# One layer's sample compressor in a two-layer transformer kernel: three half-width products for two neighbouring blocks in place of four, with the differences made by GpSimd and VectorE in turn

## Chip, cores and metric

One core of a Trainium2 chip runs the whole program as one launch. The metric is the device time of that launch in microseconds (us), lower is better. TensorE is PE below and its weight loads PEld; VectorE is DVE, ScalarE is ACT, GpSimd is POOL, SyncE is SP.

## What is computed

The program is one forward pass of a small two-layer model on 1024 prompt tokens and on 8 samples of 4 new tokens with 2048 cached positions each. The change lies in the second (odd) layer, in the part for the samples: sparse attention with compressed blocks. The cached keys and values of a sample are cut into blocks of 32 positions, one every 16, and each block goes through a small network:

```python
per = CMP_LEN // CMP_STRIDE                      # 32 // 16 = 2
n_cmp = (t - CMP_LEN) // CMP_STRIDE + 1          # 127 blocks for 2048 positions
pieces = kv[:, :CMP_STRIDE * (n_cmp + per - 1)].reshape(n, n_cmp + per - 1, CMP_STRIDE, g, hd)
blocks = jnp.concatenate([pieces[:, j:j + n_cmp] for j in range(per)], axis=2)
hid = silu(einsum('nilgd,ldf->nigf', blocks + pos_emb, w1.reshape(CMP_LEN, hd, CMP_HIDDEN)))
return einsum('nigf,fd->nigd', hid, w2)          # (n, 127, 2 groups, 64)
```

So with pieces x[i] of 16 positions, hidden block i is A x[i] + B x[i+1] plus a bias, where A and B are the two halves of w1 (each 1024 x 256), for keys and for values with weights of their own. The queries attend the compressed blocks; their probabilities choose which 64-position blocks of the cache are attended in full; a window of the last 512 positions is attended too; the three results are mixed by gates.

## The kernel before

`build` runs stages one after the other, each a set of five instruction streams (one for each engine) with semaphores between them. The stage of this change is `attend_samples_sparse` (L2886). It comes after the second layer's input projection (`project_out`, L1246 and L1259 are its products), and is followed by the prompt's attention of that layer.

**Items and steps.** The 8 samples go in 4 pairs p (PAIRS, L2888). For each pair there are two items: m = 0 compresses the keys, m = 1 the values, in the order K0 V0 K1 V1 K2 V2 K3 V3. An item has 8 steps l (KD), one for every two of the 16 positions in a piece: 2 positions x 64 dims fill the 128 rows of the contraction. The moving operand of a step is `x` of 512 columns: 2 samples x 2 groups x 128 pieces. Float32 numbers are cut into a high and a low part (`hi`, `lo`, type fp32r), and a product is three matmuls: hi x lo, lo x hi, hi x hi.

**PE.** `hidden(m, p, hh)` (L3210) is one of 16 half-steps hh of an item: l = hh // 2 is the step and c = hh % 2 the half of the 256 hidden units. It issues six matmuls of 128x512 (L3229), three for A and three for B, where B reads the same x one column further on (x[:, s:s + XW]). An item is 96 of them, the stage 768. Before step l it waits for `x_cut` (L3223); after the last half-step of a step it gives `x_used`.

**What is done between half-steps.** After each half-step PE does a piece of the other work of the pair, written out by hand: `turn(what, p, x)` transposes (ks: the selected-branch keys, L3182; win: the window's, L3186; pc, psel, pwin, pnew: probabilities, L3195 to L3207) at the slots of the tables TURNS_K and TURNS_V (L2895); `down_k`, `compressed_scores`, `scores` (into two PSUM banks by turns, L3236) at hh 1 to 4 of the V item; the sums that choose blocks at hh 7 and 8; `down_v` and `times_v` (L3282, the probabilities times the values, L3299 to L3310) at hh 1 and 4 of the next pair's K item. The streams of ACT and DVE follow the same slots in the same order, so a wait on one of them holds all that stands behind it there.

**How x is made.** Step t = item x 8 + l is made three steps ahead (`step_ahead`, L2914, at even hh). DVE turns it (`turn_x`, two transposes of 128x256, L3080) into one of two buffers `x_raw`; ACT copies it to `x_hi` (`take_x_high`, L3087), for which it waits until PE is done with the step four back (`x_used`); DVE then makes `x_lo` = x_raw - x_hi (`take_x_low`, L3093). In `take_x_low(t)` DVE first turns step t + 1, then waits for `x_high` of t.

**POOL** issues the gathers from the paged caches: eight indirect DMAs (L3032) for each item, into one of two buffers, and four (L3021) for each pair for the selected-branch keys and values. It also scales the probabilities (L3159 twice, L3160) when DVE has made the coefficients (`coef_ready`, L3572).

**The chain of the selected branch** in the V item: `select(p)` at hh 8 on DVE (choose blocks, then add the mask over 2048 scores, L3507), an exponential on ACT at hh 11 (L3427), reciprocals on DVE at hh 12 (L3572), scaling on POOL (L3159), and PE turns psel 0 and 1 at hh 15 (L3200).

**Start.** ACT and DVE cut the weights of the keys (L3393, L3522; `low_weights(0)`), and later those of the values (`low_weights(1)`); both sets stay in SBUF for the whole stage. Meanwhile PE compresses the prompt's own pieces (`comp.hidden`, L2867), and POOL issues the first gathers. The bias and the silu are one ACT instruction from PSUM for each half c (`silu`, L3367).

Of the kernel before, what the change touches and what calls it, by code (L numbers as in the profile page):

```python
# [14 lines left out]
F32 = mybir.dt.float32  # L15
# [3 lines left out]
ALU = mybir.AluOpType  # L19
# [34 lines left out]
def _constants():  # L54
# [48 lines left out]
    c, b = np.arange(NCS)[:, None], np.arange(NSL)[None, :]  # L103
# [1220 lines left out]
class SparseLoads:  # L1324


    def __init__(self, nc, ctx, constants, h, turned, mix_s, comp):
# [12 lines left out]
        self.o_stored = ctx.semaphore("ss_stored")  # L1340
        self.k_in = [c[:, :, :].rearrange("p s c -> p (s c)").rearrange("p (t g a d) -> p t g a d", t=NT, g=2, a=2) for c in self.c_in]
# [1544 lines left out]
def attend_samples_sparse(nc, constants, comp, following, h, kcmp, vcmp, pools, wins, gates, mix_s):  # L2886

    PAIRS = NB // 2  # L2888
    NKEY = PAST + NJ
    HALVES = 2 * KD  # L2890
    AHEAD, N_X = 3, 4
    XW = 4 * P
    N_STEPS = 2 * PAIRS * KD
    R2 = 2 * 64
    TURNS_K = {0: [("psel", 2), ("psel", 3)], 1: [("pwin", 0)], 2: [("pnew", 0)], 5: [("win", 0)], 6: [("win", 1)]}  # L2895
    TURNS_V = {6: [("pc", 0)], 15: [("psel", 0), ("psel", 1)]}
    for q in range(6):
        TURNS_K.setdefault(10 + q, []).append(("ks", q))
    TURNS_K[15].append(("new", 0))
    for q in range(6, 8):  # L2900
        TURNS_V.setdefault(q - 6, []).append(("ks", q))

    def turns_of(m, p, hh):

        turns = []
        for what, x in (TURNS_V if m else TURNS_K).get(hh, ()):
            if what in ("pwin", "pnew") or what == "psel" and m == 0:
                if p:
                    turns.append((what, p - 1, x))
            else:  # L2910
                turns.append((what, p, x))
        return turns

    def step_ahead(m, p, hh):  # L2914

        n = (2 * p + m) * KD + hh // 2 + AHEAD
        return n if hh % 2 == 0 and n < N_STEPS else None

    LAST_TURNS = [("psel", PAIRS - 1, 2), ("psel", PAIRS - 1, 3), ("pwin", PAIRS - 1, 0), ("pnew", PAIRS - 1, 0)]
# [6 lines left out]
    for p in range(PAIRS):  # L2926
        for m in range(2):
            for hh in range(HALVES):
                for x in turns_of(m, p, hh):
                    enter(*x)  # L2930
    for x in LAST_TURNS:
        enter(*x)
# [4 lines left out]

    def hidden_count(m, p, c):
        return (2 * p + m) * 2 + c + 1

    with Phase(nc) as ctx:
# [11 lines left out]
        x_raw = [sb(f"x_raw{b}", [P, XW]) for b in range(2)]  # L2953
# [8 lines left out]
        kc, vc = w_flat[1][:, 2048:2048 + 2 * NCS].rearrange("p (a b) -> p a b", a=2), w_flat[1][0:NCS, 3336:3592].rearrange("c (a k) -> c a k", a=2)  # L2962
# [3 lines left out]
        w_hi, w_lo = ([sb(f"{n}{m}", [P, 16, CH], F32R) for m in range(2)] for n in ("w_hi", "w_lo"))  # L2966
        x_hi, x_lo = ([sb(f"{n}{b}", [P, XW + 2], F32R) for b in range(N_X)] for n in ("x_hi", "x_lo"))
        hid = [sb(f"hid{m}", [P, 2, 2, 2, NCS]) for m in range(2)]
        ksT = [comp.lent[:, a * PAST:(a + 1) * PAST] for a in range(2)]
        newT = sb("newT", [P, 2, 2, NJ])  # L2970
        pc, pn, pcT = sb("pc", [R2, NCS]), sb("pn", [R2, NCS]), sb("pcT", [NCS, R2])
# [4 lines left out]
        o, o_cmp = following.o, sb("o_cmp", [R2, P])  # L2976
        ps_t = [ctx.enter_context(nc.psum_tensor(f"ss_ps_t{b}", [P, 512], F32)) for b in range(2)]
        ps_s = [ctx.enter_context(nc.psum_tensor(f"ss_ps_s{b}", [P, 512], F32)) for b in range(2)]
# [45 lines left out]
        def gather_items(pool, f):  # L3024
            b = f % 2
            if f >= 2:
                pool.wait_ge(x_turned, (f - 1) * KD)
            for a in range(2):
                if f == 1 and a == 1:
                    comp.landing.wait(pool)  # L3030
                for q in range(4):
# [659 lines left out]
```

## Time and profile before

| what | value |
|---|---|
| median of three runs | 1787.94 us (1786.65 to 1789.09) |
| span of the profiled execution | 1786.0 us |
| PE busy over the span | 1725.0 us |
| DVE, ACT, POOL busy | 892.8, 695.8, 418.0 us |
| the stage's products of x run from | 978.1 to 1245.1 us of the span |
| DMA | 245.31 MB, mean 137 GB/s |

The span runs from the first to the last instruction of the program; the time of a run also has what lies around it, here 1.9 us from the profile's span to the median. A row of the profile names the line of the kernel, the engine, the operation and the tiles (out<-in), with shapes as partitions x elements. PE's records overlap, since matmuls are pipelined, so the pace of a run of matmuls is read from their starts and not from their durations.

### The profile page before, as it was taken

The numbers are of one execution on the slowest core, as the hardware profiler recorded it, in microseconds if no ns is written. First come the engines' busy times: TensorE is split into PE (matmuls) and PEld (weight loads), VectorE is DVE, ScalarE is ACT, GpSimd is POOL, SyncE is SP. The second block draws the span as 40 slices with busy tenths as digits, with TensorE's granted clock in tenths as the row PEclk, the third lists the DMA queues.
The fourth block names the chain that finished last, engine by engine and source line by source line (L and its number), as shares of the span: only waits on it lengthen the run. The fifth ranks groups of instructions, "written<-read, shape, count | busy, mean of one in ns | idle before, by whom it ended". The sixth has DMA issues, their size and how long they took to land. (4 is left out here: it accounts for less than half of the span.)

```text
span 1786.0 us, 34260 instructions
## 1 busy us (share of the span) xinstructions
PE 1725.0 (97%) x13111; PEld 1412.2 (79%) x13111; DVE 892.8 (50%) x2673; ACT 695.8 (39%) x1535; POOL 418.0 (23%) x591
## 2 busy tenths in 40 slices
PE   7999999999899899999999999999799999999998
PEld 5878778678776778887789787787688888888998
DVE  5322222288456445222224555454677787778534
ACT  4200000176332323100112334233687877787413
POOL 0000000000464000000003342331365656565300
PEclk9999999999999999999999999999899999999999
DMA  5443343464889765466434442536400000000154
GB/s 211 147 171 135 141 152 111 148 225 138 258 259 287 258 227 193 116 196 206 135 98 157 161 140 92 196 110 165 119 20 25 26 26 24 22 14 8 59 163 156
DMA packets 148409, 245.31 MB, mean 137 GB/s; under 512 B 34939, under 2 KB 82808, under 8 KB 145944
## 3 DMA queue, kind: packets, MB, share of 16 engines
q1 hardware_dynamic: 132936, 198.48, 34.4%
q0 software_dynamic: 7424, 33.56, 5.5%
q10 hardware_dynamic: 7888, 11.08, 2.1%
q8 instruction: 107, 1.75, 0.4%
q14 instruction: 54, 0.44, 0.1%
HBM read 201.35 MB, written 48.77 MB: 140 GB/s over the span
## 5 line engine op out<-in xcount | busy, mean ns | idle before, releaser
L1998 POOL TENSOR_SCALAR sparse_pr<-sparse_pr,sparse_coef,sparse_gate 128x63 f32<-128x63 f32 (+8 forms) x384 | 247.1, 662 | 160.8 <-DVE sparse_coef L1938 160.8
L1884 ACT ACTIVATE sparse_pr<-sparse_pr,sparse_nmax 128x63 f32<-128x63 f32 (+8 forms) x384 | 227.7, 595 | 67.5 <-DVE sparse_nmax L1932 67.3
L1246 PE MATMUL x_acc<-x_w_hi,x_y_lo 128*128 128x512 f32 (+3 forms) x448 | 157.3, 351 | 1.6 <-DVE x_y_lo L1058 1.4
L1246 PE MATMUL x_acc<-x_w_lo,x_y_hi 128*128 128x512 f32 (+3 forms) x448 | 155.3, 347 | 0.0
L1246 PE MATMUL x_acc<-x_w_hi,x_y_hi 128*128 128x512 f32 (+3 forms) x448 | 154.9, 346 | 0.0
L511 PE MATMUL h_acc<-h_w_hi,h_y_lo 128*128 128x512 f32 x384 | 151.7, 395 | 0.8 <-DVE h_y_lo L433 0.8
L511 PE MATMUL h_acc<-h_w_lo,h_y_hi 128*128 128x512 f32 x384 | 150.1, 391 | 0.0
L511 PE MATMUL h_acc<-h_w_hi,h_y_hi 128*128 128x512 f32 x384 | 149.9, 390 | 0.0
L1805 PE MATMUL sparse_ps<-cmp_lent,ss_pieces 64*128 64x384 f32 (+3 forms) x928 | 136.6, 421 | 5.2 <-DVE sparse_part L1932 3.5
L1817 PE MATMUL sparse_ps<-constants_shared,sparse_pr 128*128 128x128 f32 x1120 | 132.9, 276 | 3.3 <-DVE sparse_nmax L1932 2.2
L458 DVE COPY cmp_w<-h_acc 128x512 f32<-128x512 f32 x48 | 33.2, 691 | 204.6 <-PE h_acc L511 204.6
L1817 PEld LDWEIGHTS sparse_ps<-constants_shared,sparse_pr 128*128 128x128 f32 x1120 | 123.0, 142 | 10.8 <-DVE sparse_nmax L1932 4.7
L1932 DVE CUSTOM_DVE_ANT_0 sparse_pr<-sparse_ps,cmp_w 128x63 f32<-128x63 f32 (+4 forms) x384 | 121.0, 369 | 17.2 <-PE sparse_ps L1805 17.0
L1845 PE MATMUL sparse_ps_o<-sparse_prT,ss_pieces 128*64 128x128 f32 x2112 | 128.6, 273 | 0.0
L3032 POOL DMA_INDIRECT ss_c_in<-in_cache_c_kcmp,cmp_quarters x32 | 34.3, 1071 | 402.2 <-POOLq L168 383.8
L1691 DVE COPY sparse_prT<-sparse_ps 128x384 f32<-128x384 f32 (+1 forms) x152 | 94.1, 621 | 58.1 <-PE sparse_ps L1817 54.5
L1845 PEld LDWEIGHTS sparse_ps_o<-sparse_prT,ss_pieces 128*64 128x64 f32 x2112 | 116.9, 137 | 3.7 <-issue 3.2
L3229 PE MATMUL ss_ps_h<-ss_x_lo,ss_w_hi 128*128 128x512 f32 x256 | 109.7, 429 | 1.0 <-ACT ss_hid L3367 1.0
L2339 POOL MEMSET ev_q_all<- 128x1024 f32 x1 | 1.0, 953 | 464.4 <-POOLq L1694 464.4
L1805 PEld LDWEIGHTS sparse_ps<-cmp_lent,ss_pieces 64*128 64x128 f32 x928 | 73.7, 188 | 40.2 <-issue 14.4
L1932 DVE CUSTOM_DVE_ANT_0 sparse_pr<-sparse_ps,cmp_w,sparse_part 128x128 f32<-128x128 f32 (+3 forms) x208 | 101.0, 526 | 4.1 <-PE sparse_ps L1805 4.1
L3229 PE MATMUL ss_ps_h<-ss_x_hi,ss_w_lo 128*128 128x512 f32 x256 | 102.4, 400 | 0.0
(406 smaller groups left out, 3474.0 us busy)
## 6 DMA issues: line engine op xcount, KB each, us to landing
h_w_side<-in_even_w_in SPq DMA_DIRECT2D x16, 896.0 KB
h<-cmp_w SPq DMA_DIRECT2D x48, 256.0 KB, 2.0
h_w_raw<-in_even_w_in SPq DMA_DIRECT2D x6, 2048.0 KB, 8.9
x_w_side<-in_odd_w_in SPq DMA_DIRECT2D x16, 716.0 KB, 6.7
cmp_lent<-in_odd_w_in SPq DMA_DIRECT2D x5, 2048.0 KB, 9.3
ev_unit<-in_cache_a_k SPq DMA_DIRECT2D x4, 2048.0 KB
ev_unit<-in_cache_a_v SPq DMA_DIRECT2D x4, 2048.0 KB
h_turned<-x_out SPq DMA_DIRECT2D x32, 256.0 KB, 2.7
```

The source lines that it names most:

```text
L458: nc.vector.tensor_copy(outb[:, b, 0:width(i)], acc[b][:, 0:width(i)]).then_inc(evacuated[b], 1)
L511: last = nc.tensor.matmul(acc[b][:, 0:width(i)], rows[:, k, t * P:(t + 1) * P], weights(cols, i)[:, k, :], start=(k == 0 and a == 0), stop ...
L1246: last = nc.tensor.matmul(acc[b][:, 0:passes[p][3]], left[:, k, t * P:(t + 1) * P], weights(right, p)[:, k, :], start=(k == 0 and a == 0), ...
L1691: ins = nc.scalar.copy(to, src) if by_act(what, x) else nc.vector.tensor_copy(to, src)
L1805: ins = nc.tensor.matmul(to[e][:, o:o + b - a], qT[i % 2][half, t * P:(t + 1) * P], rhs, start=True, stop=True)
L1817: last = nc.tensor.transpose(to[:, x:x + P], pr[:, e, at:at + P], con("ident"))
L1845: ins = nc.tensor.matmul(ps_o[e * HD:(e + 1) * HD, cols], lhs, rhs, start=br == segs[0][0] and k == s0, stop=br == segs[-1][0] and k + P > ...
L1884: nc.scalar.activation(row, row, ACT.Exp, scale=-1.0, bias=nmax[u % UB][:, e * NBR + br:e * NBR + br + 1], accum_out=lsum[u % UB][:, e * N ...
L1932: nc.vector.tensor_tensor_reduce(out=row_of(e, a, b, blocks), in0=bank("score", (c, e))[:, o:o + b - a], in1=bias, scale=1.0, scalar=so_fa ...
L1998: nc.gpsimd.tensor_scalar(row, row, one, gate[:, t, 2 * i + e, (br + 1) % 3:(br + 1) % 3 + 1], ALU.mult, ALU.mult).then_inc(scaled, 1)
L3032: pool.indirect_dma_start(out=split[b][a][:, q * 512:(q + 1) * 512], out_offset=None, in_=pools[f % 2].rearrange("r (k c) -> (r k) c", k=4 ...
L3229: ins = nc.tensor.matmul(ps_h[c][:, :], w[m][:, lw, c * P:(c + 1) * P], x[b][:, s:s + XW], start=l == 0 and s == 0 and i == 0, stop=l == K ...
```

## The change

It rewrites how the samples' hidden blocks are made, and the schedule around it.

1. Two neighbouring blocks share a product. With an even piece e = x[2j], the odd one o = x[2j+1] and the next even one e' = x[2j+2], block 2j is A(e - o) + (A+B)o, and block 2j+1 is (A+B)o + B(e' - o). So a step is `both` (kind 2, A+B times o), kind 0 (A times e - o) and kind 1 (B times e' - o), each on 256 columns, for two halves c: 18 matmuls of 128x256 in place of 12 of 128x512.
2. `turn_x` writes even and odd pieces apart. A new `differ` makes the two differences (one instruction with 512 results): on POOL for even steps, on DVE for odd ones. `x_hi` and `x_lo` have 768 columns.
3. `both` has a PSUM bank of its own; ACT copies it out (`take_both`), DVE adds it to the sums of each half (`add_parts`), and ACT's silu works in SBUF on that. `scores` is left with one PSUM bank.
4. The items' order becomes K0 K1 K2 K3 V0 V1 V2 V3. There is one set of cut weights, with three kinds. During item 3 the values' weights replace the keys' in place, step by step: SP loads two 128x256 parts (four DMAs, after the step before is cut), POOL adds them, ACT and DVE cut them.
5. The other work is placed by an explicit table; of a pair p > 0 the compressed scores come in its first item at hh 4, and the mask, exponential, coefficients and scaling at hh 8, 9, 10 and 11 of its second item, psel 0 and 1 at hh 14. `mask` is split from `select`. The sum over selected and window values is copied out (`take_acc`), and the compressed values are added items later (`times_vc`, `out`).

The columns of the constant `overlap` and the block order of the hidden rows are permuted to fit. The core of the diff:

```diff
-    XW = 4 * P
+    XP = 2 * P
+    XO_AT = XP + 8
+    E_AT = XO_AT + XP
+        cmp_item, c0 = (o, 3) if p == 0 else (e, 4)
+        at(cmp_item, c0, "cmp", p)
...
+        for x in range(5):
+            at(o, 3 + x, "scores", p, x)
+        tail = (o, 11) if p == 0 else (o, 8)
...
+        at(*later(0), "mask", p)
+        at(*later(1), "exp", p)
+        at(*later(2), "coef", p)
+        at(*later(3), "scale", p)
+        for x in range(2):
+            turn_at(*later(6), "psel", p, x)
+            turn_at(*later(7), "psel", p, 2 + x)
...
+        at(*later(10), "values", p)
...
+        at(p + 1, 1, "down_k", p)
...
+        def load_next(sp, l):
+            if l:
+                sp.wait_ge(next_cut, l)
+            fr = comp.w1_of[1].rearrange("(s b u p) f -> u b p s f", s=2, b=4, u=8)
+            for b in range(4):
+                sp.dma_start(w_next[32 * b:32 * b + 32, :, :], fr[l, b]).then_inc(next_in, 16)
...
+        def by_pool(t):
+            return t % 2 == 0
+
+        def differ(eng, t):
+            eng.wait_ge(x_turned, t + 1)
...
+            eng_of.tensor_tensor(raw[:, E_AT:E_AT + 2 * XP].rearrange("p (r c) -> p r c", r=2), after, odd, ALU.subtract).then_inc(x_diff[t % 2], 1)
...
+            act.wait_ge(x_diff[t % 2], t // 2 + 1)
...
+            nc.scalar.copy(x_hi[t % N_X][:, :], x_raw[t % 2][:, XO_AT:XO_AT + 3 * XP]).then_inc(x_high, 1)
...
+                def next_sum(l):
+                    pool.wait_ge(next_in, 64 * (l + 1))
...
+                    nc.gpsimd.tensor_tensor(w_next_sum[:, :], w_next[:, 0, :], w_next[:, 1, :], ALU.add).then_inc(next_summed, 1)
...
+                for n, hh in slots():
+                    t = step_ahead(n, hh)
+                    if t is not None and t + 1 < N_STEPS and by_pool(t + 1):
+                        differ(pool, t + 1)
...
+                    if hh >= 7 and hh < 15 and n + 2 < ITEMS:
+                        gather_quarter(pool, n + 2, hh - 7)
+                    if (n, hh) == (PAIRS, 0) or n == PAIRS - 1 and hh >= 2 and hh % 2 == 0:
+                        next_sum(KD - 1 if n == PAIRS else hh // 2 - 1)
...
+                        for c in range(2):
+                            last = product(ps_x[:, c * XP:(c + 1) * XP], 2, c, 0, c == 0, c == 1)
...
+                        product(ps_h[0][:, 0:XP], 0, 0, 1, True, False)
+                    else:
+                        last = product(ps_h[0][:, XP:2 * XP], 1, 0, 2, False, True)
...
+                        product(ps_h[1][:, 0:XP], 0, 1, 1, True, False)
+                        product(ps_h[1][:, XP:2 * XP], 1, 1, 2, False, True).then_inc(x_used, 1)
...
+                def take_both(n):
+                    act.wait_ge(both_done, n + 1)
...
+                    nc.scalar.copy(both_sb[:, :], ps_x[:, :]).then_inc(both_taken, 1)
...
+                def next_high_part(l):
+                    act.wait_ge(next_summed, l + 1)
+                    act.wait_ge(x_used, (PAIRS - 1) * KD + l + 1)
+                    nc.scalar.copy(w_hi[:, l, 0:2, :], w_next[:, :, :])
+                    nc.scalar.copy(w_hi[:, l, 2, :], w_next_sum[:, :]).then_inc(next_high, 1)
...
+                    nc.vector.tensor_tensor(to, own, both, ALU.add).then_inc(summed, 1)
+
+                def next_low_part(l):
+                    dve.wait_ge(next_high, l + 1)
+                    nc.vector.tensor_tensor(w_lo[:, l, 0:2, :], w_next[:, :, :], w_hi[:, l, 0:2, :].bitcast(F32), ALU.subtract)
+                    nc.vector.tensor_tensor(w_lo[:, l, 2, :], w_next_sum[:, :], w_hi[:, l, 2, :].bitcast(F32), ALU.subtract).then_inc(next_cut, 1)
...
+                    if (n, hh) == (PAIRS, 1) or n == PAIRS - 1 and hh >= 3 and hh % 2 == 1:
+                        next_low_part(KD - 1 if n == PAIRS else (hh - 3) // 2)
...
+                nc.vector.tensor_tensor(w_sum, first, second, ALU.add).then_inc(w_summed, 1)
+                for kind, raw in enumerate((first, second, w_sum)):
+                    dve.wait_ge(w_high, kind + 1)
+                    nc.vector.tensor_tensor(w_lo[:, :, kind, :], raw, w_hi[:, :, kind, :].bitcast(F32), ALU.subtract).then_inc(w_cut, 1)
```

A slot (n, hh) below is half-step hh of item n, n from 0 to 7 in the new order; items 2p and 2p + 1 carry the other work of pair p.

## Rows read from the trace of the kernel before

**Rows 1.** The page, busy time by engine: busy us, share of the span, instructions.
```profile
PE 1725.0 (97%) x13111; PEld 1412.2 (79%) x13111; DVE 892.8 (50%) x2673; ACT 695.8 (39%) x1535; POOL 418.0 (23%) x591
```

**Rows 2.** Busy time by stretch: the stage, a V item, a K item; clock, DMA.
```profile
978.00:1246.00 268.00, 265.13 (x1507) 204.66 (x1506) 144.62 (x382) 92.92 (x153) 85.15 (x81) 0.99 0.47 149
1010.00:1043.00 33.00, 33.00 (x162) 24.03 (x161) 19.96 (x60) 14.40 (x23) 6.49 (x6) 1.00 0.18 64
1043.00:1078.00 35.00, 34.60 (x245) 28.45 (x245) 16.38 (x38) 9.01 (x17) 16.98 (x17) 1.00 0.65 212
```

**Rows 3.** Timeline of PE: the first and last of 36 stage products in a row.
```profile
1098.60 0.40 PE L3229 MATMUL ss_ps_h<-ss_x_hi,ss_w_lo 128*128 128x512 f32 x1
...
1106.81 0.40 PE L3229 MATMUL ss_ps_h<-ss_x_lo,ss_w_hi 128*128 128x512 f32 x1
```

**Rows 4.** Timeline of PE: 20 products of 512, 27 of 304 columns; a transposes' row.
```profile
859.64 0.39 PE L1259 MATMUL x_acc<-x_y_hi,x_w_lo 128*128 128x512 f32 x1
...
863.94 0.39 PE L1259 MATMUL x_acc<-x_y_lo,x_w_hi 128*128 128x512 f32 x1
...
939.33 0.30 PE L1246 MATMUL x_acc<-x_w_lo,x_y_hi 128*128 128x304 f32 x1
...
942.92 0.30 PE L1246 MATMUL x_acc<-x_w_hi,x_y_lo 128*128 128x304 f32 x1
...
1108.23 1.04 PE L3200 MATMUL ss_ps_t<-constants_shared,ss_psel 128*128 128x128 f32 x8
```

**Rows 5.** Timeline of DVE, ACT, POOL and SP at the stage's start.
```profile
958.19 7.30 ACT L3393 CAST ss_w_hi<-cmp_w 128x2048 fp32r<-128x2048 f32 x4 [29.02 <-PEq L168]
960.46 2.78 POOL L3032 DMA_INDIRECT ss_c_in<-in_cache_c_kcmp,cmp_quarters  x1 [0.30 <-issue]
974.44 1.42 DVE L3080 STREAM_TRANSPOSE ss_x_raw<-ss_c_in 128x256 f32<-128x256 f32 x4 [9.82 <-DMA ss_c_in<-in_cache_c_kcmp,cmp_quarters]
980.23 0.95 POOL L3032 DMA_INDIRECT ss_pieces<-in_cache_c_vcmp,cmp_quarters  x1 [0.30 <-issue]
980.47 4.48 DVE L3522 TENSOR_TENSOR ss_w_lo<-cmp_w,ss_w_hi 128x2048 fp32r<-128x2048 f32 x2
981.48 4.30 POOL L3032 DMA_INDIRECT ss_pieces<-in_cache_c_vcmp,cmp_quarters  x1 [0.31 <-issue]
985.05 0.83 SPq L3012 DMA_DIRECT2D cmp_w<-in_cache_c_kwin  x2
```

**Rows 6.** Timeline: pair 1's chain from mask to PE's turn of psel.
```profile
1100.38 0.69 DVE L3507 CUSTOM_DVE_ANT_1 ss_psel<-ss_psel,cmp_w 128x512 f32<-128x512 f32 x1
...
1102.95 0.16 DVE L3511 TENSOR_REDUCE ss_nmax<-ss_mins 128x1 f32<-128x5 f32 x1
...
1103.71 0.65 DVE L3093 TENSOR_TENSOR ss_x_lo<-ss_x_raw,ss_x_hi 128x512 fp32r<-128x512 f32 x1
1104.39 0.77 DVE L3080 STREAM_TRANSPOSE ss_x_raw<-ss_c_in 128x256 f32<-128x256 f32 x2
...
1107.21 1.19 DVE L3093 TENSOR_TENSOR ss_x_lo<-ss_x_raw,ss_x_hi 128x512 fp32r<-128x512 f32 x1
...
1103.14 2.01 ACT L3427 ACTIVATE ss_psel<-ss_psel,ss_nmax 128x2052 f32<-128x2052 f32 x1 [2.50 <-DVE ss_nmax L3511]
...
1106.66 2.82 POOL L3159 TENSOR_SCALAR ss_psel<-ss_psel,ss_coef,ss_gate 128x1024 f32<-128x1024 f32 x2 [23.43 <-DVE ss_coef L3572]
```

**Rows 7.** Groups by form: POOL's two-input instructions elsewhere, and two copies of the stage.
```profile
L2326 POOL TENSOR_TENSOR ev_kdm<-ev_kd_s,constants_even 32x512 f32<-32x512 f32 x4 | 4.0, 1035 | 0.1
L2298 POOL TENSOR_TENSOR ev_m<-cmp_w,ev_cs 128x256 f32<-128x256 f32 x8 | 5.8, 730 | 17.0 <-DMA cmp_w<-h 11.4 <-PE ev_ps_a L2473 5.5
L3087 ACT CAST ss_x_hi<-ss_x_raw 128x512 fp32r<-128x512 f32 x64 | 39.3, 619 | 42.1 <-PE ss_ps_h L3229 30.4 <-DVE ss_x_raw L3080 7.6 <-issue 3.9
L3468 DVE COPY ss_psel<-ss_ps_s 128x512 f32<-128x512 f32 x8 | 5.5, 693 | 12.2 <-PE ss_ps_s L3250 12.2
```

**Rows 8.** DMA issues of the stretch 940 to 1262: KB each, median us to landing.
```profile
h<-x_out SPq DMA_DIRECT2D x5, 152.0 KB, 1.8
ss_ks_in<-in_cache_c_vsel,cmp_rows POOLq DMA_INDIRECT x8, 6.9
```

More of the change, by code:

```diff
@@ L2888, in attend_samples_sparse @@
     PAIRS = NB // 2
+    ITEMS = 2 * PAIRS
     NKEY = PAST + NJ
@@ L2903, in turns_of @@
[L2903 to L2919, printed above, removed]
+    E_AT = XO_AT + XP
@@ new lines, in attend_samples_sparse, with slots, last_slots, events @@
+    for p in range(PAIRS):
+        at(p + 1, 1, "down_k", p)
+        at(PAIRS + p + 1, 1, "down_v", p)
+        at(PAIRS + p + 1, 4, "cmp_values", p)
+        at(PAIRS + p + 1, 4, "out", p)
+    def slots():
+        return itertools.product(range(ITEMS), range(HALVES))
+    def last_slots():
+        return [(ITEMS, hh) for hh in range(HALVES)]
+    def events(n, hh):
+        return events_at.get((n, hh), ())
+    def turns_of(n, hh):
+        return turns_at.get((n, hh), ())
+    def step_ahead(n, hh):
+        t = n * KD + hh // 2 + AHEAD
+        return t if hh % 2 == 0 and t < N_STEPS else None
@@ L2925, in attend_samples_sparse @@
     enter("q", 0, 0)
[L2926 to L2932, printed above, removed]
+    for n, hh in [*slots(), *last_slots()]:
+        for x in turns_of(n, hh):
+            enter(*x)
     def bank(what, p, x):
@@ L3060, in take @@
                     eng.wait_ge(av_done, p)
-                if what == "pc":
-                    last = copy(pcT[:, :], src[0:NCS, 0:R2])
-                elif what == "psel":
+                if what == "psel":
                     last = copy(pselT[:, 4 * x:4 * x + 4, :], src[:, :].rearrange("p (c k) -> p c k", c=4))
@@ new lines, in scores_new @@
+                def scores_new(p):
+                    copied("new", p, 0)
+                    if p == 0:
+                        pe.wait_ge(cmp_probs, 1)
+                    elif p == 1:
+                        pe.wait_ge(kc_ready, 3)
+                    else:
+                        pe.wait_ge(vc_ready, 2 * p - 3)
+                    for a in range(2):
+                        half = slice(a * 64, a * 64 + 64)
+                        last = nc.tensor.matmul(ps_m[half, M_NEW], q_all[:, 2 * p + a, :], newT[:, a, :, :].rearrange("p x j -> p (x j)"),
+                                                start=True, stop=True)
+                    last.then_inc(new_scored, 1)
@@ L3258, in down_k @@
-                def down_k(p):
-                    pe.wait_ge(active, hidden_count(0, p, 1))
-                    if p:
-                        pe.wait_ge(vc_ready, p)
+                    if 5 * p + x:
+                        pe.wait_ge(s_free, 5 * p + x)
+                    for a in range(2):
+                        half, lhs = slice(a * 64, a * 64 + 64), q_all[:, 2 * p + a, :]
+                        rhs = ksT[a][:, x * 512:(x + 1) * 512] if x < 4 else kwT[a]
+                        last = nc.tensor.matmul(ps_s[half, :], lhs, rhs, start=True, stop=True)
@@ L3513, in _ @@
+                first, second = comp.w1[0][:, 0:KD, :], comp.w1[0][:, KD:2 * KD, :]
                 nc.vector.memset(q_all[:, :, :], 0.0).then_inc(q_zero, 1)
-                for b in range(N_X):
-                    nc.vector.memset(x_lo[b][:, XW:XW + 2].bitcast(F32), 0.0)
-                    last = nc.vector.memset(x_hi[b][:, XW:XW + 2].bitcast(F32), 0.0)
+                for b in range(2):
+                    last = nc.vector.memset(x_raw[b][:, XP:XO_AT], 0.0)
                 last.then_inc(pad_zeroed, 1)
-                def low_weights(m):
-                    for b in range(2):
-                        dve.wait_ge(w_high[m], b + 1)
-                        part = slice(8 * b, 8 * b + 8)
-                        nc.vector.tensor_tensor(w_lo[m][:, part, :], comp.w1[m][:, part, :], w_hi[m][:, part, :].bitcast(F32), ALU.subtract
-                                                ).then_inc(w_cut[m], 1)
```

650 lines of the change are left out of this document (367 added, 283 removed).

## The prediction

> **What bounds the kernel now.** I read the page's busy times first: PE is busy for nearly the whole span [rows 1]. As records of pipelined matmuls overlap, that only says where to look. The busy time by stretch shows the stage of the change itself, 268 us: PE is taken for 265 of them, DVE for 145, ACT for 93, POOL for 85, at full clock, in a V item as in a K item [rows 2]. So PE sets the stage's time, and a product less is time less, as long as the others keep up. What a product costs is read from the starts on PE's timeline: 36 in a row start 8.21 us apart from first to last, 0.2346 us each [rows 3]. The stage's 768 products are then 180.2 us; the other 88 us are transposes, scores, times_v and waits. Last I read the chain of pair 1 from mask to psel across the engines [rows 6], since the new schedule gives it fewer and shorter slots.
>
> **The products.** 768 of 512 columns go, 1152 of 256 come. No row has 256 columns in this number type, so I bound it. Elsewhere in the program 512 columns take 4.30 / 19 = 0.2263 us and 304 take 3.59 / 26 = 0.1381 us [rows 4], a slope of 0.424 ns a column, which gives 0.118 at 256. The stage's own pace is 0.008 above that of the other 512s; half as many columns, half of it: I take 0.122. Lower end 0.110, the pace of transposes with a 128-column weight load each (eight in 1.04 us, less the last one's 0.27) [rows 4]; upper end 0.138, the 304-column row. 1152 x 0.122 = 140.5 us: **39.7 us less** (53 to 21). A half-step of nine products is then 1.1 us, a step 2.2, where it was 2.8.
>
> **The start, +4 us.** Before, DVE's two w_lo instructions of 2.28 us run while POOL issues the first gathers, and a gather beside them takes 2.78 or 4.30 us instead of 0.95 [rows 5]. Now there are four such instructions (the sum and three kinds): two more gathers are held by some 1.5 us each, and the first x, which waited for that gather until 974.44, comes 3 us later. The first step's own chain is longer by a difference on POOL (1.1, below) and 256 more columns on ACT and DVE (0.5). PE had about 1 us to spare; `low_weights(1)`, 4.5 us of DVE just after the start, goes and lets step 1 and 2 catch up. Bounds +1 to +6.
>
> **DVE, ACT, POOL for each step.** x_lo: 0.65 [rows 6] at 512 columns and 2.28 at 2048 is 1.06 ns a column, so 0.92 for 768. ACT's x_hi: 0.62 [rows 7] at 512, 1.9 at 2048 [rows 5], so 0.83. The transposes stay 0.77; their output is scattered, which no row prices: nothing to +0.2, I take nothing, as their input was scattered already. A difference on DVE is an instruction like the old x_lo, 0.65. On POOL the nearest rows are 1.035 for 512 columns on 32 partitions and 0.73 for 256 [rows 7]; I take 1.1. Added to DVE in the stage: 64 x 0.27 + 32 x 0.65 + 16 add_parts x 0.69 + 8 next_low_part x 1.04 + copies 3, less 4.5: 56 us. 145 + 56 = 201 us, in about 258. It fits on average, beside PE, and costs nothing there; it is close in stretches with little else on PE.
>
> **Handing over between items, +2 us.** ACT's take_both at hh 14 (0.6 after both is done) stands ahead of x_hi, and DVE's add_parts behind x_lo; the first half's sum is then ready some 4.0 us after hh 14 begins, and PE needs it after 1.1 + 1.1 + 0.7 = 2.9 plus the transposes of those slots (0.9 to 1.7). Bounds 0 to +6. The ends of the stage are alike (+0.5, in this term).
>
> **The chain of the selected branch, +11 us.** For p > 0 it starts at slot (o, 8). DVE has the window's scores (one instruction like the copy of scores, 0.69 [rows 7], and small ones: 1.1), two transposes and x_lo (1.7) ahead of the mask: 2.8. The mask is 2.7 and the exponential 2.1 [rows 6]. The coefficients stand behind step 10's x_hi and x_lo: 0.83 + 0.92 + 0.16 and four hand-overs of some 0.07 make 2.2. POOL's first scaling is 1.3. Sum 11.1 us. PE turns psel after seven half-steps, 7.7 us: it waits 3.4 us, three times. In pair 0 select is ahead, but PE has eight half-steps from slot 10 on: 1 us. Before, nine slots of 1.4 us just covered it. What is queued behind this wait on PE is the next item's products, so nothing hides it. Bounds +3 (what stands ahead of the mask has run early) to +16 (POOL's gathers of slots 7 to 11, 1.25 each from 980.23 to 981.48 [rows 5], come before the scaling).
>
> **The reload of the weights in item 3, +12 us.** With one buffer `w_next`, step l's parts load only when step l - 1 is cut. A round is: four DMA issues on SP at 0.41 [rows 5], so the last starts after 1.25; landing 1.8, the row of small stores [rows 8]; the sum on POOL 0.73 [rows 7]; two copies on ACT 1.0; two subtractions on DVE 1.04; hand-overs 0.3. That is 6.1 us, while a step of PE with nothing else is 2.2. ACT, DVE and POOL wait for it in line, and silu(3, 1), which down_k at (4, 1) needs, stands behind round 6: about 3.1 + 6 x 6.1 + 1.5 = 41 us after (3, 2) begins. PE gets there by itself after 16 half-steps, 17.6, some 8 of the 10.5 us of other work that a V item has (33.0 - 96 x 0.2346) [rows 2], and the chain's wait, 3.4: 29 us. Bounds +3 (2.5 us of landing and issue, waits of that pair overlapping) to +40 (landing 6.9, the gathers' row [rows 8]; the new gathers run at that time). I take the small row's, since a load is 64 KB of 1 KB rows.
>
> **The sum.** -39.7 + 4 + 2 + 11 + 12 + 0.5 (one bank for the scores: PE waits on a copy that has a half-step to be made) = -10.2 us. The profiled span is 1786.0 and the median of the runs 1787.9, 1.9 above; against the median the forecast is 1777.7, **1778 us**. Removed at no price: silu from PSUM (ACT has 93 of 268 us), the ring of two score banks. The second reading of a weight array, 2 MB, is nothing to DMA at 149 GB/s.
>
> **POOL and DVE block each other.** The gather of 4.30 us lies beside a two-input DVE instruction, and x_lo at 1107.21 takes 1.19 instead of 0.65 beside POOL's scaling, which begins at 1106.66 and needs 2.82 for two [rows 5, 6]. By the Trainium skill (SBUF — State Buffer, section "Who interferes with whom"), a DVE instruction with two SBUF inputs and a GpSimd instruction that reads SBUF exclude each other for their whole length. The trace agrees, by 4.30 and 1.19 us. In the sum it has no term of its own but within the start; by the rule each of the 32 differences on POOL could hold DVE up by its whole length, and with no cover the forecast would be up to 32 x 1.1 = 35 us higher.
>
> **Rivals.** *VectorE sets the pace (15%).* Two steps cost DVE 2 x (0.77 + 0.92) + 0.65 = 4.0 us; with POOL's difference of 1.1 in the way once, 5.1, against 4.4 on PE. For: the blocking rows above, and that POOL's difference starts just when DVE turns to x_lo. Against: DVE can turn the next step meanwhile (one input), and PE's other work gives it 88 us. 0.35 us x 64 = 22 us, half of it inside waits already counted: +11, **1789 us**.
>
> *Slower: the reload waits for its loads (22%).* Place: the round of item 3. Each us of landing more is 6 us. My gain of 10 is gone when the landing is 3.5 us instead of 1.8. At 4.4 us it is 1793, at the gathers' 6.9, **1808 us**. For: the gathers of item 5 run in the same slots, 0.5 MB on the same 16 engines, and DMA is at 0.65 of its share in such a stretch [rows 2]. Against: POOL is held in the same chain, so the gathers are spread out.
>
> *The stalls are hidden (20%).* ACT, DVE and POOL run ahead of PE by three steps, the mask starts earlier than PE's slot, and rounds overlap with the scores' slots. Then only the start and a few us are left: -39.7 + 5, **1753 us**. For: before, DVE stood idle for 123 of the 268 us [rows 2], much of it slack. Against: the chain is serial and 6.1 > 2.2.
>
> *A product of 256 columns isn't linear (8%).* At the 304 row's 0.138 the gain is 21: **1796 us**. For: each now has its own weight load for half the columns. Against: the transposes at 0.110.
>
> *It doesn't do what it says:* near 0; the count of records will show it.
>
> **How the numbers follow.** The forecast has 35%, with its own range 1768 to 1786. Within 0.2% (3.6 us, about what can be told from no change) of 1788: most of the VectorE case and the edge of the reload's, 14%. Faster: the forecast, the hidden stalls and a little of the VectorE case, 58%. Slower: the reload, the non-linear products, 28%. The range 1750 to 1800 leaves out the far half of the reload's case and the best end of the hidden stalls.
>
> **What would show it.** Right: 1152 products at 0.122; a PE wait of about 3 us before psel in items 3, 5 and 7 that POOL's scaling ends; rounds of about 6 us in item 3, with DVE and ACT waiting for POOL's sum; DVE near 200 us in the stage; first product about 982 instead of 978.1. Wrong: PE without gaps in item 3 (the stalls are hidden); PE waits for x_lo spread over all items (VectorE); rounds over 8 us (the loads); a pace of products above 0.13.

## The result, and the profile after

The changed kernel takes **1841.8 us** (median of 4 runs) against 1788.5 for the kernel before beside it: ratio 1.0302, 95% interval 1.0287 to 1.0317. It is slower by 53 us; the forecast was 1778, with a range of 1750 to 1800. The two profiled spans are 1837.8 and 1786.0 us. The page's busy times, which answer to [rows 1]:

```profile
PE 1715.8 (93%) x13495; PEld 1432.1 (78%) x13495; DVE 980.3 (53%) x2747; ACT 726.8 (40%) x1564; POOL 483.3 (26%) x631
```

PE is busy for less time (1725.0 before), and DVE, ACT and POOL for 88, 31 and 65 us more. PE's instruction count is what the diff promises: 384 products more. The stage runs from its first product at 982.3 (978.1 before) to its last at 1295.1 (1245.1), 312.8 us instead of 267.0. Its busy times by stretch, columns as in [rows 2]:

```profile
978.00:1010.00 32.00, 21.55 (x144) 21.31 (x145) 23.56 (x39) 10.27 (x14) 20.50 (x17) 0.77 0.46 154
1010.00:1043.00 33.00, 28.89 (x194) 23.00 (x193) 24.62 (x49) 12.54 (x20) 15.66 (x14) 0.94 0.37 128
...
1078.00:1113.00 35.00, 29.26 (x181) 24.70 (x181) 24.11 (x53) 13.16 (x21) 17.67 (x15) 0.85 0.35 121
1113.00:1147.00 34.00, 15.68 (x97) 13.18 (x95) 20.89 (x40) 9.67 (x15) 17.15 (x16) 0.75 0.41 132
1147.00:1180.00 33.00, 28.30 (x222) 25.77 (x222) 22.94 (x40) 14.22 (x23) 10.62 (x10) 0.74 0.40 137
1180.00:1213.00 33.00, 28.97 (x203) 23.41 (x201) 25.47 (x54) 13.01 (x19) 18.86 (x14) 0.95 0.29 97
```

Two things are to be seen. PE has holes in every stretch, where it had next to none: over the stage it is idle for 59 us, and was for 3 before. And the stretch from 1113 to 1147, in item 3, has PE at less than half. DVE stands at 21 to 26 us in these stretches of 32 to 35, where it had 15 to 21. The granted clock is below 1 in each of them; from the stage's first product to its last it is at its lower level (1.2 GHz) for 72.7 us. Before, that was 3.7 us, at the very start. By items (from one item's first product to the next one's) the eight lengths were 30.2, 32.2, 36.3, 32.2, 36.4, 32.2, 36.2 and 31.2 us. Now they are 31.7, 37.8, 41.0, **58.5**, 39.7, 38.7, 34.4 and 30.9.

The products themselves are as forecast. PE's timeline, a run in item 3, to be held against [rows 3]:

```profile
1118.56 0.28 PE L3315 MATMUL ss_ps_h<-ss_x_hi,ss_w_lo 128*128 128x256 f32 x1
...
1123.96 0.28 PE L3315 MATMUL ss_ps_h<-ss_x_hi,ss_w_lo 128*128 128x256 f32 x1
1124.08 0.28 PE L3315 MATMUL ss_ps_h<-ss_x_hi,ss_w_hi 128*128 128x256 f32 x1
1128.04 0.58 PE L3315 MATMUL ss_ps_x<-ss_x_lo,ss_w_hi 128*128 128x256 f32 x1 [3.68 <-DVE ss_x_lo L3166]
1128.42 0.41 PE L3315 MATMUL ss_ps_x<-ss_x_hi,ss_w_lo 128*128 128x256 f32 x1
1128.63 0.41 PE L3315 MATMUL ss_ps_x<-ss_x_hi,ss_w_hi 128*128 128x256 f32 x1
```

From 1118.56 to 1123.96 there are 45 steps of 0.120 us. Then PE waits 3.7 us for x_lo, and goes on at half clock, where a product takes 0.21. The waits of the stage, by engine, line and releaser (total us, times, longest):

```profile
ACT ss_x_hi L3160 <- POOL ss_x_raw L3140: 50.0, 16, 10.1
ACT ss_w_hi L3517 <- POOL ss_w_next_sum L3224: 32.1, 7, 9.6
...
DVE ss_w_lo L3626 <- ACT ss_w_hi L3518: 20.9, 6, 7.6
...
POOL ss_w_next_sum L3224 <- DMA ss_w_next<-in_cmp_w_v: 17.0, 4, 8.5
...
PE ss_ps_t L3298 <- POOL ss_psel L3259: 15.7, 3, 10.5
...
PE ss_ps_x L3315 <- DVE ss_x_lo L3166: 9.8, 2, 6.2
...
PE ss_ps_h L3315 <- DVE ss_hid L3622: 9.6, 8, 2.0
...
PE ss_ps_t L3298 <- ACT cmp_w L3122: 5.4, 1, 5.4
...
PE ss_ps_m L3465 <- DVE ss_pcT L3117: 4.4, 3, 2.0
...
PE ss_ps_x L3315 <- ACT ss_both L3501: 4.2, 1, 4.2
```

PE's own waits, 59 us for 3, are more than the whole loss; the shorter products give part of it back. Of the 59 us, 35 are psel (the selected branch's chain), x_lo and hid (the sum of the halves); the six kinds shown make 49. Only two of them are for x_lo, one in item 0 and one in item 3; the others stand where another chain is handed over to PE. Behind them stand ACT waiting for POOL's difference and for POOL's sum of the weights, and DVE waiting for ACT: the line of the reload. The costliest groups of DVE in the stage, kept apart by form, and POOL's costliest:

```profile
L3166 DVE TENSOR_TENSOR ss_x_lo<-ss_x_raw,ss_x_hi 128x768 fp32r<-128x768 f32 x63 | 64.3, 1021 | 13.0 <-ACT ss_x_hi L3160 12.6
L3151 DVE STREAM_TRANSPOSE ss_x_raw<-ss_pieces 128x256 f32<-128x256 f32 x64 | 34.8, 619 | 0.5
L3151 DVE STREAM_TRANSPOSE ss_x_raw<-ss_c_in 128x256 f32<-128x256 f32 x60 | 33.0, 626 | 0.4
L3140 DVE TENSOR_TENSOR ss_x_raw<-ss_x_raw 128x512 f32<-128x512 f32 x31 | 21.9, 707 | 1.1
...
L3140 POOL TENSOR_TENSOR ss_x_raw<-ss_x_raw 128x512 f32<-128x512 f32 x31 | 53.1, 1713 | 95.7 <-DVE ss_x_raw L3151 95.7
```

The same two groups of DVE before, for the transposes and x_lo:

```profile
L3093 DVE TENSOR_TENSOR ss_x_lo<-ss_x_raw,ss_x_hi 128x512 fp32r<-128x512 f32 x63 | 43.3, 688 | 35.3 <-ACT ss_x_hi L3087 18.2 <-issue 17.1
L3080 DVE STREAM_TRANSPOSE ss_x_raw<-ss_pieces 128x256 f32<-128x256 f32 x64 | 24.4, 420 | 1.2 <-DMA ss_pieces<-in_cache_c_vcmp,cmp_quarters 0.7
```

A transpose went from 0.42 to 0.62 us, which the forecast priced at nothing; a step's two, which overlap a little, from 0.77 to 1.10, and 64 x 0.33 = 21 us. With it DVE has 230 us in the stage (978 to 1296), not the 201 forecast, and 145 before. POOL's difference takes 1.71 us on the mean and not 1.1.

The savings of the products are not all there either. PE's busy time in the stage fell by 11 us, from 264.5 to 253.9, though 1152 products at 0.120 us are 42 us less than 768 at 0.2346. Part of that went to the low clock: 149 of the products start at half clock, where one takes 0.213 us, and 149 x 0.093 = 14 us.

### The profile page after: what moved, and what is told of

Its sections match the earlier page's. It is cut to its first block and busy times, and to the rows that moved or that the text cites. A ratio compares the mean times of both kernels' runs of the same rounds, so it can differ in the third digit from the quotient of the medians.

```text
span 1837.8 us, 35242 instructions
## 1 busy us (share of the span) xinstructions
PE 1715.8 (93%) x13495; PEld 1432.1 (78%) x13495; DVE 980.3 (53%) x2747; ACT 726.8 (40%) x1564; POOL 483.3 (26%) x631
## 5 line engine op out<-in xcount | busy, mean ns | idle before, releaser
L3088 POOL DMA_INDIRECT ss_c_in<-in_cache_c_kcmp,cmp_quarters x16 | 20.7, 1296 | 389.1 <-POOLq L169 385.0
L1260 PE MATMUL x_acc<-x_y_hi,x_w_lo 128*128 128x512 f32 x256 | 100.6, 393 | 0.0
L1260 PE MATMUL x_acc<-x_y_lo,x_w_hi 128*128 128x512 f32 x256 | 99.8, 390 | 0.0
```

The source lines that it names most:

```text
L1260: last = nc.tensor.matmul(acc[b][:, :], weights(left, p)[:, k, cols], right[:, k, tokens], start=(k == 0 and a == 0), stop=(k == KD - 1 an ...
L3088: pool.indirect_dma_start(out=split[b][a][:, q * 512:(q + 1) * 512], out_offset=None, in_=pools[m].rearrange("r (k c) -> (r k) c", k=4), i ...
```

## The experiments

All ratios are to the kernel before, run beside the experiment; differences between kernels are differences of these ratios times 1788 us. A ratio's 95% interval is about 0.3% to either side, 5 us, in e1 to e4 and e6 to e8, and about 0.2% in the others. Where the profiled spans, each from one execution, give another size than the ratios, their difference stands in brackets.

**Differences and reload.** e1 moves work, e2 and e4 leave work out, e3 does both.

```
e1:  def by_pool(t): return t % 2 == 0    ->  return False
e2:  load_next, next_sum, next_high_part, next_low_part: not called
e3:  e1 and e2
e4:  differ(...): not called; x_hi waits for x_turned alone
```

> The changed kernel with all 64 differences on DVE, none on POOL. Theory A (POOL's share of the differences is a large part of the loss: ACT stood 50 us waiting for them, each is 1.84 us long and stands in line behind gathers, scalings and sums): the changed kernel's 1841.8 us falls by 15 to 35, to some 1807 to 1827, and DVE, with 22 us more to do, does not set the pace. Rival B (DVE sets the pace; POOL only relieved it): the time rises by 5 to 20, to 1847 to 1862. Rival C (the reload in item 3 is nearly all of it): within 5 us of 1842.

> The changed kernel without the reload of item 3: the values are compressed with the keys' weights (that part of the result is left wrong, the work of the products is the same), and no load, sum or cutting of weights is made. Item 3 took 58.5 us beside 41.0, 39.7 for its like (items 2 and 4), so theory C (reload): 1841.8 falls by 18 to 25 us, to about 1820. If POOL's differences only show up there as well, less: by 5 to 12. Either way it stays above the 1788 of before, if the other items' excess (5 to 10 us each over 28) has another cause.

> Both edits at once: all differences on DVE, and no reload (values compressed with the keys' weights). If the two costs are separate and add, the sum of the two gains: about 1842 - 20 - 22 = 1800. If they are one cost seen twice (POOL blocked), no better than the better of the two. If DVE sets the pace without POOL, above the run without the reload alone.

> The changed kernel with the differences left out altogether (x_hi and x_lo of those columns are made from a constant; the hidden blocks are then wrong), the reload kept. Tells what all differences cost together, DVE's 22 us and POOL's 55: theory A says nearly the gain of moving them to DVE plus 5 to 10 us, 1800 to 1815; theory C says 1835 to 1842.

Measured: e1 1841.1 (1.0300), e2 1813.7 (1.0147), e3 1818.1 (1.0171), e4 1812.3 (1.0139). Which engine makes the differences is no matter: e1 gains 4.8 us in item 0 (26.9 us for 31.7) and loses it again in the later ones. That is what rival C named, but its reason, that the reload is nearly all, is refuted by e4. e3 isn't better than e2, where two separate gains would have given 1800. The differences' presence costs **29 us** (1.0302 to 1.0139; spans 27), of which 8.5 lie in item 0 (31.7 to 23.2); the reload costs **28 us** (1.0302 to 1.0147; spans 26), a little above theory C's 18 to 25. In e2 item 3 falls from 58.5 to 38.2 us. The wait of PE for psel remains there:

```profile
PE ss_ps_t L3294 <- POOL ss_psel L3255: 9.5, 3, 4.4
```

These are 4.4 us in items 3 and 5 and 0.7 in item 7, where the forecast had 3.4 in each, and there is none in item 1, where it had 1: 9.5 us in place of 11. In the full kernel the same wait is 15.7, as the one in item 3 is 10.5 long. In e4, with the reload, it is 10.1, and in e2, without it, 4.4: so it is the reload that stretches it.

**What is left without both, and two smaller suspects.**

```
e5:  e2 and e4
e6:  to = x_raw[t % 2][:, a * XO_AT:a * XO_AT + XP]   # even and odd pieces not parted
e7:  20 spare transposes on PE ahead of the wait for psel
e8:  the copies "ks", "win", "psel" out of PSUM all on ScalarE
```

> The changed kernel without the differences and without the reload (both parts of the computation left out as before). The reload cost 28 us and the differences 29.5, whichever engine made them. If they are separate costs, 1842 - 28 - 29 = 1785 us, 3 below the kernel before; if they share a bound (DVE's total, or the clock that falls when PE idles), more than 1790. PE's own work would allow some 1745, so what is left over 1745 is neither of the two.

> The changed kernel whose transposes write their output in rows of 32 side by side again, and not scattered to the even and odd halves (the pairing of the pieces is then wrong). In the changed kernel two transposes take 1.10 us where they took 0.77. Theory D (DVE's work for each step is the pace: 1.10 + 0.95 + 0.69 / 2 and blocks, 2.4 to 2.7 us, against 2.15 on PE): 64 x 0.33 = 21 us less on DVE bring 12 to 21 us, 1821 to 1830. Rival (the waits are chains through all engines, DVE has slack): under 5 us. And if the transposes stay at 1.10, the scatter isn't what slowed them.

> The changed kernel with 20 spare transposes (2.2 us) on PE ahead of each of the four waits for the first psel, to keep PE active in waits of 3 to 11 us. The granted clock is at half for 68 us of the stage, in none of it before. Theory E (the fallen clock is a cost of its own): half-clock time shrinks by 10 to 25 us and the time by 3 to 8 us. Rival (the clock does not matter, since PE waits anyway): the time is the same or up to 5 us more, the spare work itself.

> The changed kernel with all copies of transposed tiles (ks, win, psel) on ACT, where DVE made every other one: 28 copies of 0.69 us, 19 us, leave DVE, and ACT gets 16. Theory D (DVE's total is the pace): 8 to 19 us less, 1823 to 1834. Rival F (waits in line on ACT for x_hi's inputs bind): more, up to 10 us, since ACT's copies then stand behind its waits.

Measured: e5 1793.1 (1.0025), e6 1829.7 (1.0215), e7 1840.1 (1.0273), e8 1825.8 (1.0193). Without both the kernel is still no faster than before, so they aren't the whole loss. Together they give 50 us, not 29 + 28; the intervals are too wide to say whether these 7 us are real. The scattered writing costs 16 us (spans 10); DVE's share of the three kinds of copies costs 19 us (spans 13). These are the gains that theory D had for both, and neither edit touches a product. The copies on DVE are not new: the kernel before has them too.

The clock is the other suspect, and e7 doesn't decide it. It takes 14 us off the time at half clock (72.7 to 58.9), PE is busy for 43.5 us of that time instead of 52.2, and the ratio moves by less than its interval (0.0029 for 0.0030), the span not at all (1837.7). Theory E expected 3 to 8 us, which this interval can't exclude. In the changed kernel each of the nine low stretches after the start begins inside a wait of PE of more than 1 us, or at most 1.6 us behind one: the low clock follows the waits. What it can cost at the most is bounded: PE was busy for 52.2 of the 72.7 us, and 0.093 of each 0.213 us is 23 us. That is not the 53 us of the loss, but it is not nothing either.

**All four taken out, and a better order.** e10 to e12 compute everything.

```
e9:   e2, e4, e6 and e8 together
e10:  rounds of the reload at steps 3, 6, 10, 13, 17, 20, 24, 27 of items 3 and 4
      (was: one every two half-steps of item 3)
e11:  e10 and e8
e12:  e11, and by_pool(t): return t % 2 == 0 and t > KD
```

> Leaves out the differences (the upper half of each product's columns reads what was left there), the reload of the weights (V is made with K's), and the scatter in the transposed writes (so the samples pair wrongly); the three kinds of copies that the two engines shared are ScalarE's alone. Theory (VectorE's work per step covers the gain of the products): this frees VectorE of about 0.7 + 0.4 us per step beside run e5, and the time falls from 1793 us to 1755 to 1770; the stage comes near to 1152 products x 0.120 = 138 us less waits, and the items fall to 26 to 31 us each. Rival (the products themselves or the clock set what is left): 1785 to 1795, items as in e5 (31 to 37 us).

> Complete computation; only the order is changed: the eight rounds in which the V weights take the place of K's come every three to four steps over two items, not every two steps in one item. Theory (the 28 us that the reload cost are its rounds waiting in line: ScalarE for GpSimd's sum, GpSimd for VectorE and the load, TensorE for them all): 12 to 25 us less than the changed kernel, 1817 to 1830 us, with items 3 and 4 (58.5 and 39.7 us) falling to 43 to 48 us each. Rival (the rounds' own work on VectorE and ScalarE, 0.7 to 1.1 us each, is the cost and only moves with them): 1838 to 1844 us, the two items' sum stays at 96 to 98 us.

> Complete computation; e10's order of the rounds, and the three shared kinds of copies on ScalarE alone, as in e8. Theory (VectorE's share of the copies and the rounds in line are two separate costs): both gains add up, e10's and e8's 16 us, so 1802 to 1815 us. Rival (both relieve the same waits of item 3, since e8 already took 4 us from it): no more than 5 us below the better of the two, 1818 to 1826 us.

> Complete computation; e11, and the first nine steps' differences all on VectorE, so that none stands behind GpSimd's gathers at the start. Theory: item 0 falls by 3 to 5 us as it did in e1 (31.7 to 26.9 us), the time to 3 to 5 us below e11. Rival (VectorE then is late in item 1, as e1's sum of items did not fall): within 1.5 us of e11.

The word "steps" in e10's expectation means half-steps. Measured: e9 1778.7 (0.9957, 0.9940 to 0.9974), e10 1832.5 (1.0252, 1.0234 to 1.0271), e11 1824.2 (1.0210), e12 1818.1 (1.0171, 1.0153 to 1.0189).

e9 is the only run here that beats the kernel before, by 8 us. It falls between what was expected of it (1755 to 1770) and the rival (1785 to 1795). Its expectation counted 1.1 us of DVE per step less than e5; DVE's busy time in the stage fell from 185.2 to 153.2 us, which is 0.5 per step. e10 gives 9 us (spans 6.5), less than the 12 expected: items 3 and 4 fall from 98.2 to 89.0 us, and ACT's wait for POOL's sum goes from 32.1 to 17.0:

```profile
ACT ss_w_hi L3521 <- POOL ss_w_next_sum L3228: 17.0, 4, 7.6
...
DVE ss_w_lo L3630 <- ACT ss_w_hi L3522: 16.8, 4, 6.0
```

So about a third of the reload's 28 us comes from how densely the rounds stand; the other two thirds stay when they are spread, and no run parts their work from their waits. e11 gains 7.5 us over e10 (spans 10), where e8 alone had 19 (spans 13): the two reliefs overlap in part, and the time is the rival's (1818 to 1826). The start in e12 gives 7 us (spans 4), more than the 3 to 5 expected; item 0 falls by 6.9 (31.0 to 24.1 us). There POOL's eight gathers stood ahead of the difference of step 6. Timeline of the changed kernel there:

```profile
1000.73 0.95 POOL L3088 DMA_INDIRECT ss_pieces<-in_cache_c_kcmp,cmp_quarters  x1 [0.30 <-issue]
1001.69 1.27 POOL L3140 TENSOR_TENSOR ss_x_raw<-ss_x_raw 128x512 f32<-128x512 f32 x1
1002.99 1.56 ACT L3160 CAST ss_x_hi<-ss_x_raw 128x768 fp32r<-128x768 f32 x2 [10.12 <-POOL ss_x_raw L3140]
...
1003.86 0.96 DVE L3166 TENSOR_TENSOR ss_x_lo<-ss_x_raw,ss_x_hi 128x768 fp32r<-128x768 f32 x1 [6.96 <-ACT ss_x_hi L3160]
...
1004.87 0.58 PE L3315 MATMUL ss_ps_x<-ss_x_lo,ss_w_hi 128*128 128x256 f32 x1 [6.17 <-DVE ss_x_lo L3166]
```

Gathers from 990.9 to 1001.7, then the difference, and PE has waited 6.2 us.

**The same extra work beside either kind of product.** The last pair asks whether DVE's load as such is the cost. b1 is the kernel before, e13 is e9; in both, turn_x makes its two transposes twice. (Edit shortened.)

```
             for _ in range(2):
                 for a in range(2): ... nc.vector.transpose(...)
                 if _ == 0: last.then_inc(x_first, 1); dve.wait_ge(x_first, n + 1)
```

> The kernel before, with each step's two transposes made twice over (the same values written again; the second pair waits for the first). That gives VectorE 64 x 0.84 = 54 us more work in the stage, a little more than the change gives it. Theory (this work costs nothing where a step's products fill TensorE for 2.8 us): at most 6 us more than before, 1788 to 1794 us, and TensorE at full clock through the stage. Rival (VectorE's work costs in any order of the stage, since each step is a chain through it): 1800 to 1815 us.

> Run e9 (differences, reload, scattered writes left out, the copies on ScalarE) with the same doubling of the transposes: 0.84 us more on VectorE per step. Theory (beside products of 1.7 us a step the same work sets the pace in the long stretches): 15 to 30 us more than e9's 1779, so 1794 to 1809 us, with TensorE at half clock for 15 us or more. Rival (the changed kernel's costs come from the hand-overs between the engines and not from VectorE's load): within 6 us of e9, 1776 to 1785 us.

Measured: b1 1802.5 (1.0079, 1.0062 to 1.0095), e13 1801.1 (1.0074, 1.0057 to 1.0091). The doubling adds 48 us to DVE's busy time in the stage of b1 and 47 in e13, not 54, as a step's transposes overlap a little. In the order of before, the work was expected to be free and costs 14 us: the rival's figure. Beside e9's products it costs 21 us by the ratios (22 by the medians), the theory's figure. By the intervals of about 3 and 4 us these two could still be near each other. Without item 0 they part: in items 1 to 7 the kernel before goes from 236.8 to 244.9 us, **+8**, and e9 from 227.6 to 248.9, **+21**, for 41 and 40 us of DVE. (The profiled execution of e9 is the fastest of its six, 3 us below their median, so the 21 may be 18.) The busy times of two stretches of the kernel before with the doubling:

```profile
1010.00:1043.00 33.00, 32.00 (x155) 22.89 (x154) 24.37 (x75) 12.97 (x21) 1.89 (x2) 1.00 0.20 71
1043.00:1078.00 35.00, 32.56 (x234) 26.60 (x233) 23.02 (x54) 11.03 (x19) 18.05 (x18) 1.00 0.50 158
```

DVE is at 24.4 of 33 us there, as in the changed kernel in the same stretch (24.6), but PE is at 32.0 and not at 28.9. Where b1 lost its time stands in PE's waits, and x_lo is not among them:

```profile
PE ss_ps_t L3205 <- POOL ss_psel L3164: 5.4, 3, 1.8
PE ss_ps_t L3191 <- DMA cmp_w<-in_cache_c_kwin: 4.2, 1, 4.2
```

The first is the chain of the selected branch, three times 1.8 us, which had no wait before. The second lies in item 0: SP issues that load only when DVE has cut the weights, at 987.1 in place of 985.1. In items 1 to 7 b1 has 7 us more of waits than the kernel before and no time at half clock; e13 has 14 us more of waits than e9 and 13 us more at half clock, which is up to 6 us. These parts make 7 of the 8 us and about 20 of the 21.

So a microsecond on DVE costs about 0.2 us in the kernel before and about 0.5 in e9. That the length of the products makes this difference is the likely reason, but the two kernels also differ in their schedule, and no run parts the two.

## Why the prediction was wrong

**Right: the products.** 0.120 us where 0.122 was taken, at the full clock, from two rows of other shapes. The 8% rival of a non-linear product is out. **Right: the start, number and mechanism.** First product at 982.3 against "about 982"; the first x is turned from 977.20, 2.8 us later than before, where 3 was taken. What item 0 then loses to POOL's order was not in that term. **Nearly right: the chain of the selected branch**, 9.5 us against 11 in the run without the reload, as 4.4, 4.4 and 0.7. **Right: the count.** The change does what it says.

**Wrong, the step that failed first: "It fits on average, beside PE, and costs nothing there".** Work on DVE was costed by whether its sum fits in the stage, 201 us in 258. It did not cost nothing: the differences 29 us, the scattered writing 10 to 16, the copies 13 to 19 (not to be added up). Taken with the reload they make 62 us (1.0302 to 0.9957). Of these the forecast had 12, for the reload, so 50 us of the miss of 64 are found there; with the reload already out (e2 to e9) DVE's part is still 34. Three things were wrong in that step.
- The average says little. A step is one line through DVE (transposes), DVE or POOL (difference), ACT (x_hi), DVE (x_lo), PE, and x_raw has only two buffers. The same queues carry the other chains, of psel, hid and the probabilities, and each piece of work on DVE moves what stands behind it. PE then waits where such a chain reaches it. Run b1 shows that this was so even before: 99% PE and 54% DVE looked like slack, and 48 us of idle work cost 14.
- The forecast's own count for two steps was 4.0 to 5.1 us of DVE against 4.4 of PE, in the rival "VectorE sets the pace". With after's durations two steps are 2 x 1.10 + 2 x 0.95 + 0.69 = 4.8 us without any wait on POOL. The rival named the right engine and was given 15% and 11 us, where DVE's part is 34. But its sign, waits of PE for x_lo spread over all items, did not come: there are two, 9.8 us of 59. DVE's load shows at the hand-overs.
- "Their output is scattered, which no row prices: nothing to +0.2, I take nothing": it was 0.33 for the pair, beyond the upper end. The bound had no row behind it.

**Too small: handing over between items.** +2 was forecast, with bounds of 0 to +6. PE waits 9.6 us for hid, once in each of items 1 to 7 and a second time in item 4, and once 4.2 us for the copy of `both`; before, the like of it was one wait of 1.0 us. In e9 the two are 2.4 and 2.7 us. So most of this goes with the work that e9 takes out, and is not to be added to the 50.

**Wrong in size: the reload.** +12 was forecast, 28 measured. POOL's eight sums start at 1101.0, 1110.6, 1122.4, 1130.5, 1137.6, 1147.0, 1154.7 and 1160.8 us. The last six intervals have a mean of 8.4 us, not 6.1; 6 x 2.3 = 14 us, and 12 + 14 = 26. The terms of the round were right: the landing has a median of 2.0 in this stretch (1.8 taken), sum 0.73, ACT 1.0, DVE 1.03. What was left out is that the engines have other work when a round comes. Timeline of one round, POOL and then DVE:

```profile
1122.39 0.73 POOL L3224 TENSOR_TENSOR ss_w_next_sum<-ss_w_next 128x256 f32<-128x256 f32 x1 [8.55 <-DMA ss_w_next<-in_cmp_w_v]
...
1127.28 1.84 POOL L3140 TENSOR_TENSOR ss_x_raw<-ss_x_raw 128x512 f32<-128x512 f32 x1 [3.04 <-DVE ss_x_raw L3151]
1129.27 1.24 POOL L3088 DMA_INDIRECT ss_pieces<-in_cache_c_vcmp,cmp_quarters  x1
1130.53 0.73 POOL L3224 TENSOR_TENSOR ss_w_next_sum<-ss_w_next 128x256 f32<-128x256 f32 x1
```

```profile
1127.91 1.76 DVE L3675 CUSTOM_DVE_ANT_1 ss_psel<-ss_psel,cmp_w 128x512 f32<-128x512 f32 x1
...
1129.60 0.68 DVE L3675 CUSTOM_DVE_ANT_1 ss_psel<-ss_psel,cmp_w 128x512 f32<-128x512 f32 x1
...
1130.21 1.61 DVE L3675 CUSTOM_DVE_ANT_1 ss_psel<-ss_psel,cmp_w 128x512 f32<-128x512 f32 x1
```

The round at 1122.39 waited 8.55 us for its load (the longest landing is 7.6, once: this is the rival of the slow landing, for one round of eight). The sign that the forecast gave for that rival, rounds over 8 us, came true without it: 8.4 on the mean, with a median landing of 2.0. The next sum stands behind a difference and a gather. The weights' w_lo then stands behind the mask, whose parts take 1.76 and 1.61 us in place of 0.68.

**The blocking.** These rows say it again: the mask (two inputs) is slow just while POOL's difference (from 1127.28) or POOL's sum (from 1130.53) runs, and each of the two slow parts ends about 0.55 us after POOL's instruction. POOL is held as well: 24 of its 32 differences begin about 0.24 us after an x_lo of DVE and take 1.84 us; the other eight take 1.27 (as at 1001.69, above). By the Trainium skill (SBUF — State Buffer, section "Who interferes with whom") the two exclude each other for their whole length; the trace agrees with it. The forecast's "up to 35 us" for the 32 differences and the 29 measured are alike by luck. The price of the blocking can be read: POOL's differences are 24 x 0.57 = 14 us longer than alone, and DVE's x_lo and mask have means of 1.02 and 0.88 us where e1, with no difference on POOL, has 0.95 and 0.72, which is 64 x 0.07 + 16 x 0.16 = 7 us. And e1 is no faster. What a difference on POOL loses to the blocking and its longer time, one on DVE loses by its own 0.7 us.

**What stays open.** With all four removed the forecast's other terms give 1764 us (1786.0 - 39.7 + 4 + 2 + 11 + 0.5) and e9's span is 1773.6. About 10 us are not assigned, and up to 7 of them may be the half clock, at which PE is busy for 15 us in e9; by the last pair, x_lo's 0.95 in place of 0.69 in every step is a candidate (64 x 0.27 us at 0.5 is 9 us), but this wasn't tried alone. A second buffer for the reloaded weights wasn't tried either. Whether the half clock has a price of its own is bounded above, at 23 us in the changed kernel, and not measured.

## What to carry to other kernels

A gain on the bounding engine is safe only as far as the others keep up step by step. Write down, for one step, each engine's work in the order in which its queue does it, and follow the line through the buffers: a sum over the stage (201 of 258 us) is no cover. When an engine looks idle for half of the time, it costs one small run to find out: double a piece of its work and read the time. Here that run on the kernel before gives 0.2 to 0.3 us per us added, before anything is built. With the 85 us that DVE has more it would have said 17 to 25 us: enough to turn the forecast's gain of 10 around, though not to foresee the whole loss. And an exchange of matrix work for elementwise work (one product in four less, at 768 columns of elementwise work for 512) should be counted in the currency of the engine that pays.

## What the runs showed of the hardware

- A product of 256 columns, with a 128 x 128 weight load each, starts every 0.120 us at the full clock (2.4 GHz) and every 0.213 at the half; one of 512 columns takes 0.235 at the full clock. Half the columns take 51% of the time.
- A 128x256 transpose on VectorE takes 0.42 us with its output in rows of 32 side by side and 0.62 with even and odd elements written to two halves (0.42 again in e6).
- GpSimd's two-input difference of 128x512 takes 1.27 us alone and 1.84 when it begins during a two-input instruction of VectorE (24 of 32); VectorE's own takes 0.69. The other way round, a part of the mask on VectorE takes 1.76 us in place of 0.68 when GpSimd came first.
- In the changed kernel each of nine stretches at half clock, 3.4 to 17.1 us long, began inside a wait of PE of more than 1 us or at most 1.6 us behind one. In e7 PE ran at half clock for 58.9 us of the stage instead of 72.7, with 80 more transposes, and no gain could be told from noise.
